# Reordering one round of a sparse-attention pipeline on VectorE, TensorE and ScalarE

## What is computed

```python
l_s = jnp.einsum('bgqtd,bgtsd->bgqts', qb, k_g).astype(F32) * scale + b_s
p_s = _masked_softmax(l_s, (d_s >= 0)[:, :, None])
o_s = jnp.einsum('bgqts,bgtsd->bgqtd', p_s.astype(dt), v_g)
...
p_w = _masked_softmax(l_w, valid_w)
o_w = jnp.einsum('bgqts,bgsd->bgqtd', p_w.astype(dt), v_wb)
return (gb[..., 0:1] * o_c + gb[..., 1:2] * o_s + gb[..., 2:3] * o_w).astype(dt)
```

## Time and profile before

| | |
|---|---|
| median of 3 runs | 1313.7 us (1313.5 to 1313.7) |
| the profiled execution | 1313.48 us |
| its span in the profile | 1311.7 us |
| TensorE busy | 1297.2 us, 99% |
| VectorE busy | 1091.5 us, 83% |
| ScalarE busy | 801.1 us, 61% |
| GpSimd busy | 140.5 us, 11% |
| share of TensorE in the chain that ended last | 92% |
| scores of heads 0 and 1 to values of heads 30 and 31 | 559.31 to 603.58 us |

### The profile page before, as it was taken

How to read it: one execution, slowest core, us unless ns; L and a number is a source line. 1 busy time by engine, 2 the same in 40 slices (tenths; PEclk the granted TensorE clock), 3 DMA queues, 4 the chain that set the end, 5 groups by cost and what they waited for, 6 DMA issues and landing times.

```text
span 1311.7 us, 18774 instructions
## 1 busy us (share of the span) xinstructions
PE 1297.2 (99%) x7012; PEld 1094.3 (83%) x7012; DVE 1091.5 (83%) x1324; ACT 801.1 (61%) x1056; POOL 140.5 (11%) x212
## 2 busy tenths in 40 slices
PE   9999999999999999999999999999999999999997
PEld 6978888888878889977878888878889988887886
DVE  6977887777999874578999979999876988999985
ACT  6674665565666644585676655666646854566661
POOL 5420000000000100183000000000000001100000
PEclk9999999999999999999999999999999999999999
DMA  9535766666698666515689868698755434779860
GB/s 316 173 96 173 232 206 192 192 200 226 209 315 277 192 217 209 189 22 201 201 259 286 269 206 296 166 328 280 202 180 183 155 102 153 283 216 310 278 182 33
DMA packets 160785, 275.53 MB, mean 210 GB/s; under 512 B 7297, under 2 KB 105874, under 8 KB 156610
## 3 DMA queue, kind: packets, MB, share of 16 engines
q1 hardware_dynamic: 150512, 226.51, 49.9%
q0 software_dynamic: 9904, 46.85, 16.1%
q10 hardware_dynamic: 290, 1.11, 0.2%
HBM read 238.24 MB, written 1.07 MB: 182 GB/s over the span
## 4 chain that ended last, share of the span: by engine, by line
PE 92%; DVE 5%; issue 2%; ACT 1%; DVEq 0%; POOL 0%; ACTq 0%
PE ps L913 18%; PE ps L915 18%; PE ps L914 18%; PE ps L1588 5%; PE ps L735 3%; PE ps L737 3%; PE ps L736 3%; PE ps L1590 3%; PE ps L936 3%; PE ps L937 3%; PE ps L943 2%; DVE wlo L682 2%; PE ps L3189 1%; PE ps L1954 1%; PE ps L1096 1%
## 5 line engine op out<-in xcount | busy, mean ns | idle before, releaser
L643 DVE TENSOR_TENSOR wlo<-raw,whi 128x1024 fp32r<-128x1024 f32 x230 | 273.6, 1223 | 45.7 <-ACT whi L633 44.6
L671 ACT ACTIVATE whi<-arena 128x2048 fp32r<-128x2048 f32 x112 | 214.6, 1916 | 98.1 <-PE ps L915 95.5
L633 ACT ACTIVATE whi<-raw 128x1024 fp32r<-128x1024 f32 x230 | 232.0, 1053 | 63.1 <-PE ps L915 46.0
L682 DVE TENSOR_TENSOR wlo<-arena,whi 128x2048 fp32r<-128x2048 f32 x112 | 255.7, 2286 | 13.8 <-ACT whi L671 12.8
L913 PE MATMUL ps<-whi,acts 128*128 128x512 f32 x456 | 180.7, 396 | 0.0
L915 PE MATMUL ps<-wlo,acts 128*128 128x512 f32 x456 | 177.8, 390 | 0.0
L914 PE MATMUL ps<-whi,acts 128*128 128x512 f32 x456 | 177.7, 390 | 0.0
L913 PE MATMUL ps<-whi,ghi 128*128 128x512 f32 x272 | 106.5, 392 | 0.0
L915 PE MATMUL ps<-wlo,ghi 128*128 128x512 f32 x272 | 106.1, 390 | 0.0
L914 PE MATMUL ps<-whi,glo 128*128 128x512 f32 x272 | 105.9, 389 | 0.0
L913 PE MATMUL ps<-whi,s_hi 128*128 128x512 f32 x256 | 102.2, 399 | 3.6 <-DVE wlo L682 3.6
(11 more groups left out here) (465 smaller groups left out, 2667.0 us busy)
## 6 DMA issues: line engine op xcount, KB each, us to landing
raw<-ffn_w_down SPq DMA_DIRECT2D x88, 512.0 KB, 10.0
arena<-ffn_w_gate SPq DMA_DIRECT2D x32, 1024.0 KB, 8.2
arena<-ffn_w_up SPq DMA_DIRECT2D x32, 1024.0 KB, 7.8
arena<-arena POOLq DMA_DIRECT2D x32, 1024.0 KB, 7.7
raw<-w_up SPq DMA_DIRECT2D x44, 512.0 KB, 4.5
raw<-ffn_w_gate SPq DMA_DIRECT2D x24, 512.0 KB, 5.1
raw<-ffn_w_up SPq DMA_DIRECT2D x24, 512.0 KB, 6.0
raw<-w_down SPq DMA_DIRECT2D x22, 512.0 KB, 3.9
```

The lines of the kernel that those rows point to most:

```text
L633: act.activation(split_half(w_slots(slot)[0], mode), raw_half(h), ACT.Copy).then_inc(hi_ready, 1)
L643: dve.tensor_tensor(lo, raw_half(h), hi.bitcast(F32), ALU.subtract).then_inc(lo_ready, 1)
L671: act.activation(hi, src, ACT.Copy).then_inc(hi_ready, 2)
L682: dve.tensor_tensor(lo, src, hi.bitcast(F32), ALU.subtract).then_inc(lo_ready, 2)
```

## The change

Three orders within a round are altered. No instruction is added or removed, and no semaphore, buffer or wait is changed.

- VectorE: the second maximum of a round moves ahead of the reciprocal of the odd head of the round before.
- TensorE: in rounds 3 to 16 the values come ahead of the turn; rounds 2, 17 and 18 stay as they are.
- ScalarE: the copy of the even head's turned weights moves from ahead of the round's two exponentials to behind them.

```diff
@@ pe_attention
                 for i in (2 * j, 2 * j + 1):
                     if i in between:
                         between[i](pe)
+                if 3 <= j <= n // 2:
+                    values(2 * j - 6)
                 if 2 <= j < n // 2 + 2:
                     pe_turn_weights(pe, u0, 2 * j - 4, turn_order, buf)
                     pe_turn_weights(pe, u0, 2 * j - 3, turn_order, buf)
-                if j >= 3:
+                if j > n // 2:
                     values(2 * j - 6)
@@ dve_attention
             for j in range(n // 2):
                 dve_maximum(dve, u0, 2 * j, add(2 * j), buf)
+                dve_maximum(dve, u0, 2 * j + 1, add(2 * j + 1), buf)
                 if j >= 1:
                     dve_reciprocal(dve, u0, 2 * j - 1, buf)
-                dve_maximum(dve, u0, 2 * j + 1, add(2 * j + 1), buf)
                 if j >= 2:
                     dve_turned_weights(dve, u0, 2 * j - 3)
                 dve_reciprocal(dve, u0, 2 * j, buf)
@@ act_attention
             for j in range(n // 2):
+                act_exponent(act, u0, 2 * j, buf)
+                act_exponent(act, u0, 2 * j + 1, buf)
                 if j >= 2:
                     act_turned_weights(act, u0, 2 * j - 4)
-                act_exponent(act, u0, 2 * j, buf)
-                act_exponent(act, u0, 2 * j + 1, buf)
```

## The result

The changed kernel takes 1330.24 us (1330.10 to 1330.39) against 1313.6 us for the kernel before on the same chip: 16.6 us more, a ratio of 1.0128 with a 95% interval of 1.0116 to 1.0141. Forecast were 1327.3 us, 13.8 more, and a range of 1324.5 to 1331.0. Direction and mechanism came out as written. The forecast time was 2.9 us too low, and the measured one lies 2.2 us above 1328.0, the upper end that the sum's own bounds gave.

What follows compares the result with a forecast made beforehand. TensorE was taken to bound the kernel, busy 1297.2 of 1311.7 us. Start -0.07, middle +13.13 and end +0.75 made 13.8 us on 1313.5: 1327.3 us, own range 1324.6 to 1328.0, stated range 1324.5 to 1331.

Steps and rivals of the forecast that it cites:

- TensorE bounds the layer, the round is its own issue: Before the change, a steady round of the layer is 2.485 us, with nothing in it but TensorE's own issue.
- The second maximum waits for the very head that the round turns: On VectorE, head 2j+1's maximum needs the slot of head 2j-4, turned in that round; it starts 0.72 us later.
- The ring: Loop of turn, maximum, exponential, copy, values and next turn, without overlap; its sum, 3.44 us, is the round against 2.485.
- turn to its reader 0.58: Step from the start of TensorE's turn to the start of what reads its first half: 0.58 us.
- the middle: From values of heads 0 and 1 to those of 26 and 27: 13 rounds of 3.44, 44.72 us against 31.59, +13.13.
- +0.05 for a hand-over of another kind: Bound on the step from copy to TensorE, 0.06 in place of 0.01 us: 13 x 0.05 = +0.7 us.
- Start -0.07: First values of the layer: head 0's copy ends at 568.37, a change of -0.07 us.
- end +0.75: From the values of heads 26 and 27 to the layer's end: 4.30 us in place of 3.55, +0.75.
- VectorE's edit 0: Second maximum ahead of the reciprocal: cost 0, hidden by TensorE's round; GpSimd's scaling needs the reciprocal over a round later.
- ScalarE's edit closes the ring only together with the others: Head 2j-4's copy waits behind head 2j+1's exponential; the three edits together close a loop of 3.44 us.
- The delay is passed on whole: Behind the layer TensorE's work hangs on the last values, so all 13.8 us stay; at most 2.7 us might be recovered.
- The clock rival: TensorE's pauses in the layer drop its clock to 1.2 GHz: 1342.9 us for all 13 rounds, 1332.5 for a third; 7%.

## Why the prediction came out, and what was mis-sized

- *TensorE bounds the layer, the round is its own issue.* Right: the six-slot kernel with TensorE's edit is back within 0.1 us of 2.485 in all rounds but one, though its order is another.
- *The second maximum waits for the very head that the round turns.* Right, and the cause of most of it: 13 waits of L1999 for L1968 in the changed kernel, and 11.1 us gone with a sixth slot.
- *The ring, 3.44 us.* The right members, shown by the timeline and by two changes that acted on it as counted (one slot more, and 0.14 less in one step). Its size was 3.62. The term that was mis-sized is "turn to its reader 0.58". I took it from a copy on ScalarE; the reader in the ring is a maximum on VectorE with three waits, of which the one that binds sits on an instruction of its own: 0.72. That is 13 x 0.14 = 1.8 of the 2.4 us missing in the middle. The rest is 0.04 a round, spread over the other steps. My bounds held +0.05 for a hand-over of another kind, not this.
- *The range.* Its upper end of 1331 was right by luck. The sum's own bounds ended at 1328.0, and what put 1330.24 inside was room left for a clock that falls in a few rounds. No clock fell; the mis-sized step used that room up.
- *Start -0.07, end +0.75.* Measured +0.03 (568.82 - 559.66 against 568.44 - 559.31) and +0.91. At the start nearly all of the 0.10 is the last step: from the copy (568.25) to the first value matmul (568.82) it is 0.57, where the sum had 0.50. The second maximum of round 2 does wait for its turn with the longer step (565.69 to 566.42), but it has ended 0.3 before its exponential can start, so that costs nothing:

```profile
566.98 0.09 DVE L1999 DVE_READ_ACCUMULATOR2_ANT arena<- 128x1 f32 x1
...
567.37 0.39 ACT L2040 ACTIVATE ffn_buf<-ffn_buf,arena 128x128 f32<-128x128 f32 x1
...
568.25 0.47 ACT L2049 ACTIVATE probT_n<-ps 128x384 f32<-128x384 f32 x1
...
568.82 0.87 PE L1934 MATMUL ps<-probT_n,arena 128*64 128x256 f32 x8 [0.74 <-issue]
```

  At the end most of the 0.16 is the turn of head 30, which starts 1.19 after that of head 28 (617.92 against 616.73), not 1.08.
- *VectorE's edit 0.* Right for the rounds, and for the three edits together: 0.12 us in the layer beside TensorE's edit, nothing beside both. Alone it costs some 0.4 us as the pipeline drains, through the late scaling that the prediction had called hidden; in the kernel's time that can't be told from nothing.
- *ScalarE's edit closes the ring only together with the others.* Not right: it has a ring of its own, of 2.88 us, through the bank that the turn waits for. For the sum this made no difference, since the larger ring held.
- *The delay is passed on whole.* Right: 708.1 us behind the layer in both.
- *The clock rival.* It did not come true: no round with its two short pauses was slowed in any kernel. A kernel with nearly the same rounds lost 1.2 us to the clock, but behind the one long pause at its end.
- *Total.* 13.8 forecast; 16.46 in the layer and 0.35 in unchanged code ahead of it.

## What to carry to other kernels

In a software pipeline that one engine fills, reordering that engine's round is free only as long as no buffer is handed back later than its next user asks for it. Look for each buffer's count, not only for the data: five slots at two heads a round make the second head of a round wait for the first head turned in the same round. Write down the loop of hand-overs and add up its steps; the round is the larger of that sum and the engine's own work, and a wait that closes the loop costs its full excess in every round. And let the wait that comes last in time be the one that the instruction itself carries: here that took 0.13 to 0.14 us off each round, though most of it was lost again to the clock at the end.

## What the runs showed of the hardware

- A wait that sits on an instruction of its own in VectorE's queue costs 0.13 to 0.14 us when it is the last to be met: the maximum starts 0.59 against 0.72 after the transposes start. Which wait that is followed, in both kernels, the order in which they are written: the first rides on the instruction. TensorE seems to have the same at a lower price. In ScalarE's edit alone it is 0.58 from the copy to the turn, where by the trace the wait for the copy sits on an instruction of its own (L1928); in the changed kernel it is 0.51 from the copy to the values, whose first weight load carries that wait itself. That was not tried by itself.
- The granted clock held at 1.00 while TensorE stood for 0.4 to 0.55 us twice in every 3.62, over a quarter of the time, for 47 us. It fell to 0.50 behind one pause of 1.8 us in one kernel, in both of its profiles, and not behind pauses of 1.9 to 2.0 us in three others; and once, in another kernel, at 56 us with no pause of TensorE in the 12 us ahead. Why it falls is open.
